# New orders in the hand-over from the output projection to the FFN, and split weights kept for both token halves

## The chip, the cores and the metric

The kernel runs on one core of one Trainium2 chip. The metric is the device time of one execution in microseconds. The core has a matrix engine (PE in the profile, with its weight loads as PEld), a vector engine (DVE), a scalar engine (ACT), a general engine (POOL) and a queue that issues the DMAs (SP). Each runs its own list of instructions in order. They meet only at semaphores, so an instruction that waits holds up all that stands behind it on its engine.

## The reference, cut to what matters

One decoder layer for a prompt of 1024 new tokens (with 16 meta tokens before them) and 8 sample tokens: retention and convolution run in parallel, and one output projection joins them. What follows is where the change lies:

```
mix = concatenate([ret_out, conv_out]) @ w_out          # 1024 x 1024
h   = h + rms_norm(mix, n_mix_post)
xf  = rms_norm(h, n_ffn_pre)
gate, up = split(xf @ w_ffn_in)                         # 1024 x 2*2816
h   = h + rms_norm((silu(gate) * up) @ w_ffn_out, n_ffn_post)
```

Everything is float32.

## The kernel before

**Products.** A float32 product is made of three passes: each operand is split into a rounded part (hi) and a remainder (lo), and hi·hi, hi·lo and lo·hi are added up (`three_pass`, L461 to L463). ACT makes a hi part by a copy, DVE (or POOL) the lo part by a subtraction. The FFN's product of a 2x2 block is made with seven products in place of eight, of sums and differences of blocks. So there are seven weight operands and seven operands of x for each pair of weight blocks. The sums of the weights are made by POOL from the raw weights (`w_sums`).

**Stages.** The FFN runs in 11 groups. Group 0 starts while the output projection still works, and this stage, the hand-over, is what the change touches. The 1032 output tokens are nine tiles: 0 to 7 of 128 tokens, and 8, the samples. Their order is 0, 1, 8, 2, 3, 4, 5, 6, 7, and o is a tile's place in it. The FFN treats the tokens as two halves: ss=0 is made of tiles 0 to 3 and half the samples, ss=1 of tiles 4 to 7 and the rest.

For each tile:

- PE makes the projection, `out_tok(t, 0)` and `out_tok(t, 1)`: 24 matmuls of 512 columns each. (Tiles 0, 1 and 8 come by another way, `mix_back`.)
- ACT squares and sums it (`mix_sum`, L1204). DVE makes mean plus epsilon (`mix_var`, L1703), POOL the power -0.5 (`mix_power`, L688), and DVE scales (`mix_scale`, L1712) into the only buffer `m_sc`.
- POOL adds it to h (`h_add`, L860) in a ring of three buffers, `h_ring`, which SP fills with x ahead and stores to memory afterwards. SP loads the tile at place o+2 only when `h_scale` of place o-1 is done.
- ACT sums the squares of h (`h_sum`, L1204), DVE makes `h_var` (L1719), POOL `h_power` (L688), and DVE `h_scale` (L1727) into the only buffer `h_sc`.
- PE transposes (`h_back`, L2299) into the only PSUM pair for that. It waits until the tile before has been read out of there.
- ACT copies x to `x_a` and splits it (L1234 to L1249), DVE makes the lo parts and two of the sums (`x_own_lo`, L1739 to L1749, and `x_sums_lo`, L1758), and POOL the other two sums (`x_sums_14`, L775 and L776). An even tile is only copied and split. The sums are made when its odd partner is there.

**The order** is written out by hand, one list for each engine. After the last projection PE runs `h_back(6)`, then the seven products of group 0 for ss=0 (k = -7 to -1), `h_back(7)`, and the same seven for ss=1 (k = 0 to 6). Products 7 to 13 (both halves) belong to the second weight block (e=1) and 14 to 20 to the down projection.

**Weights.** The seven split operands of e=0 are made for k = -7 to -1 in a ring of four slots, and then once more for k = 0 to 6 in a ring of seven (`w_op_hi` on ACT, L1265, and `w_op_lo` on DVE, L1763). The raw weights of e=1 of group 0 have buffers of their own, `f_first`, and so have their sums, `t_first`. SP loads them after the last projection (L598).

**Between products** there are partial results: `u2` (L1777) is needed by the product with p=3, and `u3` (L1783), the second gate (L1787), the second up half (L1794) and their product (L1800), the first up half (L1806) and its product (L1815) stand between the weight splits on DVE.

## Time and profile before

| | us |
|---|---|
| median of the runs (three: 1169.47, 1173.04, 1173.50) | 1173.04 |
| the profiled execution, its time | 1173.48 |
| its span | 1171.7 |
| PE busy | 1138.5 |
| DVE busy | 805.4 |
| POOL busy | 610.4 |
| ACT busy | 440.7 |

PE works 97% of the span, so the time can only fall where PE waits or where it runs at the lower of its two clocks. The profile's forty slices show a dip of PE in slices 14 to 17, which is 380 to 500 us. There lies the hand-over. Times of day below are microseconds from the span's start.

### The profile page before, as it was taken

How to read it: one execution, taken by the hardware profiler on the slowest of the kernel's cores; microseconds unless marked ns; L12 is line 12 of the kernel's file. 1: busy time of each engine (PE TensorE's matmuls, PEld its weight loads, DVE VectorE, ACT ScalarE, POOL GpSimd, SP SyncE). 2: the span in 40 equal slices, each digit the busy share in tenths (PEclk: the TensorE clock that was granted, in tenths of full speed). 3: DMA queues.
4: the chain of work that ended last, by engine and by line, in shares of the span. 5: the costliest groups of instructions: out<-in, count | busy, mean ns of one | idle time of the engine just before them, and what ended most of it. 6: DMA issues, size and time to landing. Idle time of an engine off the chain costs nothing.

```text
span 1171.7 us, 22760 instructions
## 1 busy us (share of the span) xinstructions
PE 1138.5 (97%) x8585; PEld 1116.4 (95%) x8585; DVE 805.4 (69%) x1243; ACT 440.7 (38%) x803; POOL 610.4 (52%) x458
## 2 busy tenths in 40 slices
PE   8999999999999988699999999999999999999997
PEld 8999999999999867699999999999999999999997
DVE  6368999954566365768685859594949586867646
ACT  6444444233346434442423333333333333333313
POOL 2066888304123464546565647474747373737416
PEclk9999999999999998899999999999999999999999
DMA  9311111111162431112121111212121212121134
GB/s 316 95 39 53 39 52 55 37 51 53 37 179 64 158 125 54 54 55 73 37 71 37 49 59 37 71 36 72 36 72 36 72 36 72 36 70 37 54 144 165
DMA packets 102360, 84.51 MB, mean 72 GB/s; under 512 B 2723, under 2 KB 89379, under 8 KB 102299
## 3 DMA queue, kind: packets, MB, share of 16 engines
q1 hardware_dynamic: 102258, 83.68, 22.9%
q8 instruction: 36, 0.59, 0.2%
q14 instruction: 18, 0.14, 0.0%
q10 hardware_dynamic: 48, 0.10, 0.0%
HBM read 72.86 MB, written 11.38 MB: 72 GB/s over the span
## 4 chain that ended last, share of the span: by engine, by line
PE 80%; POOL 6%; DVE 6%; issue 4%; DMA 2%; ACT 1%; DVEq 0%; POOLq 0%; SPq 0%; ACTq 0%
PE ps L461 25%; PE ps L463 25%; PE ps L462 24%; DVE w_ring L1763 2%; DMA f_raw<-in_w_ffn_in 2%; POOL st L688 1%; POOL o_last L933 1%; PE ps L2097 1%; DVE ffn_acc L1941 1%; POOL f_sum L804 1%; POOL f_sum L802 1%; POOL h_ring L860 1%; PE ps L2225 1%; POOL f_raw L805 1%; PE ps L2169 1%
## 5 line engine op out<-in xcount | busy, mean ns | idle before, releaser
L1941 DVE TENSOR_TENSOR ffn_acc<-ps,ffn_acc 128x516 f32<-128x516 f32 x264 | 183.7, 696 | 8.7 <-PE ps L463 2.9
L461 PE MATMUL ps<-xn_hi,w_hi 128*128 128x350 f32 (+2 forms) x576 | 187.2, 325 | 0.9 <-DVE xn_lo L1445 0.9
L463 PE MATMUL ps<-xn_lo,w_hi 128*128 128x350 f32 (+2 forms) x576 | 185.2, 322 | 0.0
L462 PE MATMUL ps<-xn_hi,w_lo 128*128 128x350 f32 (+2 forms) x576 | 185.0, 321 | 0.0
L461 PE MATMUL ps<-x_both,w_ring 128*128 128x256 f32 x616 | 173.3, 281 | 6.9 <-DVE e_s L1777 4.2
L461 PE MATMUL ps<-x_hi,w_ring 128*128 128x260 f32 x616 | 175.2, 284 | 4.6 <-DVE e_s L1777 2.5
L463 PE MATMUL ps<-x_lo,w_ring 128*128 128x260 f32 x616 | 174.6, 283 | 0.0
L462 PE MATMUL ps<-x_hi,w_ring 128*128 128x260 f32 x616 | 174.6, 283 | 0.0
L462 PE MATMUL ps<-x_both,w_ring 128*128 128x256 f32 x616 | 174.5, 283 | 0.0
L463 PE MATMUL ps<-x_both,w_ring 128*128 128x256 f32 x616 | 174.3, 283 | 0.0
L461 PE MATMUL ps<-act_hi,w_ring 128*128 128x258 f32 x560 | 158.2, 282 | 0.5 <-DVE e_s L1806 0.4
L462 PE MATMUL ps<-act_hi,w_ring 128*128 128x258 f32 x560 | 158.0, 282 | 0.0
L463 PE MATMUL ps<-act_lo,w_ring 128*128 128x258 f32 x560 | 157.9, 282 | 0.0
L1763 DVE TENSOR_TENSOR w_ring<-f_raw,w_ring 128x512 fp32r<-128x512 f32 x140 | 108.9, 796 | 55.8 <-ACT w_ring L1265 55.1
L1265 ACT CAST w_ring<-f_raw 128x512 fp32r<-128x512 f32 x160 | 96.9, 618 | 123.4 <-POOL f_raw L813 83.2
L688 POOL TENSOR_TENSOR st<-st,nhalf 128x1 f32<-128x1 f32 (+4 forms) x54 | 37.6, 697 | 184.6 <-DVE st L1663 59.9
L461 PEld LDWEIGHTS ps<-x_both,w_ring 128*128 128x128 f32 x616 | 117.6, 191 | 7.4 <-DVE w_ring L1763 4.5
L461 PEld LDWEIGHTS ps<-x_hi,w_ring 128*128 128x128 f32 x616 | 116.9, 190 | 6.5 <-DVE w_ring L1763 5.0
L463 PEld LDWEIGHTS ps<-x_both,w_ring 128*128 128x128 f32 x616 | 117.3, 190 | 0.0
L462 PEld LDWEIGHTS ps<-x_both,w_ring 128*128 128x128 f32 x616 | 116.7, 189 | 0.0
L463 PEld LDWEIGHTS ps<-x_lo,w_ring 128*128 128x128 f32 x616 | 116.6, 189 | 0.0
L462 PEld LDWEIGHTS ps<-x_hi,w_ring 128*128 128x128 f32 x616 | 116.5, 189 | 0.0
(272 smaller groups left out, 2714.1 us busy)
## 6 DMA issues: line engine op xcount, KB each, us to landing
f_raw<-in_w_ffn_in SPq DMA_DIRECT2D x42, 512.0 KB, 3.9
raw<-in_w_in SPq DMA_DIRECT2D x24, 512.0 KB, 3.7
f_raw<-in_w_ffn_out SPq DMA_DIRECT2D x22, 512.0 KB, 3.5
x_st<-in_x_prompt SPq DMA_DIRECT2D x8, 512.0 KB, 7.7
h_ring<-in_x_prompt SPq DMA_DIRECT2D x8, 512.0 KB, 3.8
h_scratch<-h_ring SPq DMA_DIRECT2D x8, 512.0 KB, 3.9
h_fin<-h_scratch SPq DMA_DIRECT2D x8, 512.0 KB
out<-o_last SPq DMA_DIRECT2D x7, 512.0 KB
```

Of the source, the lines that this page charges most:

```text
L461: nc.tensor.matmul(out, hi, mhi, start=first, stop=False, skip_group_check=resumes)
L462: nc.tensor.matmul(out, lo, mhi, start=False, stop=False, skip_group_check=resumes)
L463: return nc.tensor.matmul(out, hi, mlo, start=False, stop=last, skip_group_check=resumes)
L688: g.tensor_tensor(dst, src, nhalf[0:src.shape[0], 0:src.shape[1]], ALU.pow).then_inc(done, 1)
L802: g.tensor_tensor(t3, up[:, half:D], up[:, 0:half], ALU.subtract).then_inc(s_T, 1)
L804: g.tensor_tensor(t2, t3, gate[:, 0:half], ALU.add).then_inc(s_T, 1)
L805: g.tensor_tensor(up[:, 0:half], up[:, 0:half], gate[:, 0:half], ALU.subtract).then_inc(s_T, 1)
L860: g.tensor_tensor(h[o % 3][0:n, :], h[o % 3][0:n, :], m_sc[0:n, :], ALU.add).then_inc(s_h, 1)
L933: g.tensor_tensor(o_last[0:n, t, :], o_last[0:n, t, :], h_fin[t][0:n, :], ALU.add).then_inc(s_y, 1)
L1265: s.copy(w_slot(k, 0), w_op(k, first)).then_inc(s_ohi, 1)
L1763: v.tensor_tensor(w_slot(k, 1), w_op(k, first), w_slot(k, 0).bitcast(F32), ALU.subtract).then_inc(s_olo, 1)
L1941: v.tensor_tensor(a, tile_banks(i), a, ALU.add).then_inc(s_acc, 1)
```

## The change

It leaves all groups from the second on as they are, and changes the hand-over:

- All four lists (PE, DVE, ACT, POOL) are in new orders. The steps on x are cut into smaller ones (`x_first`, `x_even`, `x_odd`; `x_even_lo`, `x_sum_3`, `x_sum_2`, `x_odd_lo`; `x_sum_1`, `x_sum_4`) so that each can have its own place. `MIX_SUMS_BEFORE` and `H_SUMS_BEFORE` hold how many sums come ahead of each.
- PE: the first product stands ahead of `h_back(6)`, and the last two of ss=0 stand behind `h_back(7)`.
- The seven split operands of e=0 are kept for both halves: four in the ring's slots, three in `w_keep`. Products 0 to 6 use them again. Seven copies on ACT and seven subtractions on DVE fall away.
- `f_first` and `t_first` are gone. The raw weights of e=1 come by the ordinary buffers, and their loads wait until the seventh lo part is made.
- The four sums of the first weights (`first_sum`) stand singly between the early additions on POOL.
- The waits on the gains stand one step later. `gate2` and `up2` are steps of their own. The splits for k = 8 to 12 come between the last partial results of e=0.

```diff
-MIX_AHEAD = 3
-CATCH_UP = {7: (10, 11), 8: (12, 13), 9: (14, 15), 10: (16,), 11: (17,), 12: (18,), 13: (19,)}
+KEEP = 7 - MIX_RING
+MIX_SUMS_BEFORE = (3, 3, 4, 5, 5, 6, 7, 8, 9)
+H_SUMS_BEFORE = (0, 0, 0, 2, 3, 5, 6, 7, 8)
...
+        def w_slot(k, part, first=False):
+            if first and k < 7:
+                p = k % 7
+                return (w_ring[p] if p < MIX_RING else w_keep[p - MIX_RING])[:, part, :]
+            return w_ring[k % RING][:, part, :]
...
-                if o == 7:
-                    sp.wait_ge(s_mT, 9)
-                    sp.wait_ge(fraw_in[0], 16)
-                    load_first(0)
-                    load_first(1)
...
                     sp.wait_ge(s_olo, splits(0, 6))
+                    load_gate_up(2, 0, 1, 0)
+                    load_gate_up(0, 0, 1, 1)
                     load_down_half(1, 0, 0)
...
             def p1_copy(g, e, first, k):
                 for ss in subs_of(first, k):
                     act.wait_ge(s_pd, products(g, k, ss, first))
+                    if first and e:
+                        act.wait_ge(s_p2, ss + 1)
...
             out_tok(7, 0)
             out_tok(7, 1)
+            product(0, -7, True)
             h_back(6)
-            for k in range(-7, 0):
-                product(0, k, True)
+            product(0, -6, True)
+            product(0, -5, True)
+            product(0, -4, True)
+            product(0, -3, True)
             h_back(7)
+            product(0, -2, True)
+            product(0, -1, True)
+            product(0, 0, True)
```

The order on DVE before, from the lo part of the fifth weight operand to the last `h_scale` (names: `w_ring` and `w_keep` hold split weights, `e_s` partial results, `x_both` the split x of the second half, `x_f` its sums, `m_sc` the scaled projection, `h_sc` the scaled h):

```order
L1763 TENSOR_TENSOR w_ring_107<-f_raw,w_ring_107 128x512 [waits ffn_w_hi]
L1777 TENSOR_TENSOR e_s_60<-ps,e_s_59 128x260 [waits p1_copied,ffn_products_done]
L1763 TENSOR_TENSOR w_ring_108<-f_raw,w_ring_108 128x512 [waits ffn_w_hi]
L1758 TENSOR_TENSOR x_both_58<-x_f_55,x_both_57 128x1024 [waits x_sums_hi,x_sums_1_4]
L1763 TENSOR_TENSOR w_ring_109<-f_raw,w_ring_109 128x512 [waits ffn_w_hi]
L1783 TENSOR_TENSOR e_s_61<-ps,e_s_59 128x260 [waits ffn_products_done]
L1787 TENSOR_TENSOR e_s_59<-ps,e_s_61 128x260 [waits u3_done]
L1719 TENSOR_SCALAR st<-st 128x1 [waits h_sumsq]
L1763 TENSOR_TENSOR w_ring_106<-f_raw,w_ring_106 128x512 [waits ffn_w_hi]
L1794 TENSOR_TENSOR e_s_61<-ps,e_s_61 128x260 [waits ffn_products_done]
L1800 TENSOR_TENSOR ffn_acc<-e_s_61,e_s_59 128x260 [waits up2_done,gate2_silu]
L1727 SCALAR_TENSOR_TENSOR h_sc<-h_ring_83,st,gain_fp 128x1024 [waits h_transposed,h_rstd]
```

The same place in the change:

```order
L1753 TENSOR_SCALAR st<-st 128x1 [waits mix_sumsq]
L1832 TENSOR_TENSOR w_ring_110<-f_sum,w_ring_110 128x512 [waits ffn_w_hi]
L1832 TENSOR_TENSOR w_keep_78<-f_raw,w_keep_78 128x512 [waits ffn_w_hi]
L1764 SCALAR_TENSOR_TENSOR m_sc<-ps,st,gain_mp 128x1024 [waits h_done,mix_rstd]
L1846 TENSOR_TENSOR e_s_60<-ps,e_s_59 128x260 [waits p1_copied,ffn_products_done]
L1792 TENSOR_TENSOR x_both_58<-ps,x_both_57 128x1024 [waits x_first_half_copied,xf_hi_done]
L1852 TENSOR_TENSOR e_s_61<-ps,e_s_59 128x260 [waits ffn_products_done]
L1827 TENSOR_TENSOR x_both_58<-x_f_55,x_both_57 128x1024 [waits x_sums_hi,x_sums_1_4]
L1771 TENSOR_SCALAR st<-st 128x1 [waits h_sumsq]
L1858 TENSOR_TENSOR e_s_59<-ps,e_s_61 128x260 [waits u3_done]
L1866 TENSOR_TENSOR e_s_61<-ps,e_s_61 128x260 [waits u3_done,ffn_products_done]
L1779 SCALAR_TENSOR_TENSOR h_sc<-h_ring_84,st,gain_fp 128x1024 [waits h_transposed,h_rstd]
```

The wait on the squares of h (`h_sumsq`) had six rows of weight splits, sums and partial results between it and the last x split (`x_both_58<-x_f_55`). Now it stands right behind that split, and two partial results stand between it and the `h_sc` row. The splits of the last two operands (`w_keep_79`, `w_keep_80`) follow after.

DVE before, from the first sums of the last tile on:

```order
L1758 TENSOR_TENSOR x_both_58<-x_f_56,x_both_57 128x1024 [waits x_sums_hi]
L1758 TENSOR_TENSOR x_both_58<-x_f_56,x_both_57 128x1024 [waits x_sums_hi,x_sums_1_4]
L1806 TENSOR_TENSOR e_s_60<-ps,e_s_60 128x260 [waits ffn_products_done]
L1815 TENSOR_TENSOR e_s_60<-e_s_60,ffn_acc 128x260 [waits up1_done,gate1_silu]
L1763 TENSOR_TENSOR w_ring_109<-f_sum,w_ring_109 128x512 [waits ffn_w_hi]
L1763 TENSOR_TENSOR w_ring_110<-f_raw,w_ring_110 128x512 [waits ffn_w_hi]
L1777 TENSOR_TENSOR e_s_60<-ps,e_s_59 128x256 [waits p1_copied,ffn_products_done]
L1763 TENSOR_TENSOR w_ring_111<-f_raw,w_ring_111 128x512 [waits ffn_w_hi]
L1763 TENSOR_TENSOR w_ring_112<-f_raw,w_ring_112 128x512 [waits ffn_w_hi]
L1783 TENSOR_TENSOR e_s_61<-ps,e_s_59 128x256 [waits ffn_products_done]
```

The same place in the change:

```order
L1827 TENSOR_TENSOR x_both_58<-x_f_56,x_both_57 128x1024 [waits x_sums_hi]
L1881 TENSOR_TENSOR e_s_60<-ps,e_s_60 128x260 [waits ffn_products_done]
L1846 TENSOR_TENSOR e_s_60<-ps,e_s_59 128x256 [waits p1_copied,ffn_products_done]
L1827 TENSOR_TENSOR x_both_58<-x_f_56,x_both_57 128x1024 [waits x_sums_hi,x_sums_1_4]
L1832 TENSOR_TENSOR w_ring_107<-f_raw,w_ring_107 128x512 [waits ffn_w_hi]
L1852 TENSOR_TENSOR e_s_61<-ps,e_s_59 128x256 [waits ffn_products_done]
L1858 TENSOR_TENSOR e_s_59<-ps,e_s_61 128x256 [waits u3_done]
L1889 TENSOR_TENSOR e_s_60<-e_s_60,ffn_acc 128x260 [waits up1_done,gate1_silu]
L1866 TENSOR_TENSOR e_s_61<-ps,e_s_61 128x256 [waits u3_done,ffn_products_done]
L1832 TENSOR_TENSOR w_ring_108<-f_sum,w_ring_108 128x512 [waits ffn_w_hi]
L1881 TENSOR_TENSOR e_s_60<-ps,e_s_60 128x256 [waits ffn_products_done]
```

The partial result for the fourth product of the second half (`e_s_60<-ps,e_s_59 128x256`) stood behind two weight splits and the second x split. Now it stands ahead of that x split, and no weight split of e=0 is left.

DVE at the start of the hand-over, before:

```order
L1712 SCALAR_TENSOR_TENSOR m_sc<-ps,st,gain_mp 128x1024 [waits mix_rstd]
L1712 SCALAR_TENSOR_TENSOR m_sc<-ps,st,gain_mp 128x1024 [waits h_done,mix_rstd]
L1719 TENSOR_SCALAR st<-st 128x1 [waits h_sumsq]
L1727 SCALAR_TENSOR_TENSOR h_sc<-h_ring_81,st,gain_fp 128x1024 [waits h_rstd]
L1712 SCALAR_TENSOR_TENSOR m_sc<-ps,st,gain_mp 8x1024 [waits h_done,mix_rstd]
L1719 TENSOR_SCALAR st<-st 128x1 [waits h_sumsq]
L1703 TENSOR_SCALAR st<-st 128x1 [waits mix_sumsq]
L1719 TENSOR_SCALAR st<-st 8x1 [waits h_sumsq]
L1712 SCALAR_TENSOR_TENSOR m_sc<-ps,st,gain_mp 128x1024 [waits h_done,mix_rstd]
```

And in the change:

```order
L1764 SCALAR_TENSOR_TENSOR m_sc<-ps,st,gain_mp 128x1024 [waits gains_in,mix_rstd]
L1753 TENSOR_SCALAR st<-st 128x1 [waits mix_sumsq]
L1753 TENSOR_SCALAR st<-st 8x1 [waits mix_sumsq]
L1764 SCALAR_TENSOR_TENSOR m_sc<-ps,st,gain_mp 128x1024 [waits h_done,mix_rstd]
L1771 TENSOR_SCALAR st<-st 128x1 [waits h_sumsq]
L1764 SCALAR_TENSOR_TENSOR m_sc<-ps,st,gain_mp 8x1024 [waits h_done,mix_rstd]
L1771 TENSOR_SCALAR st<-st 128x1 [waits h_sumsq]
L1753 TENSOR_SCALAR st<-st 128x1 [waits mix_sumsq]
L1764 SCALAR_TENSOR_TENSOR m_sc<-ps,st,gain_mp 128x1024 [waits h_done,mix_rstd]
L1771 TENSOR_SCALAR st<-st 8x1 [waits h_sumsq]
L1779 SCALAR_TENSOR_TENSOR h_sc<-h_ring_82,st,gain_fp 128x1024 [waits h_rstd]
```

The first `h_sc` row stood behind two `m_sc` rows, and now stands behind four.

## Rows read from the trace of the kernel before

**Rows 1.** The page: PE's busy time, and its clock in forty slices (9: full).

```profile
PE 1138.5 (97%) x8585; PEld 1116.4 (95%) x8585; DVE 805.4 (69%) x1243; ACT 440.7 (38%) x803; POOL 610.4 (52%) x458
...
PEclk9999999999999998899999999999999999999999
```

**Rows 2.** Busy time by stretch: us, then PE, PEld, DVE, ACT, POOL; clock; DMA.

```profile
384.40:406.50 22.10, 22.10 (x99) 18.05 (x97) 9.17 (x12) 7.72 (x14) 13.38 (x12) 1.00 0.53 170
406.50:443.30 36.80, 32.37 (x162) 26.11 (x160) 23.61 (x29) 13.63 (x24) 22.72 (x17) 1.00 0.31 100
443.30:468.40 25.10, 21.22 (x89) 17.25 (x89) 13.13 (x16) 11.20 (x17) 10.45 (x9) 0.86 0.17 63
468.40:504.40 36.00, 26.58 (x185) 25.95 (x184) 26.88 (x37) 16.35 (x29) 14.74 (x9) 0.86 0.18 59
504.40:545.00 40.60, 39.66 (x331) 39.31 (x330) 32.58 (x51) 13.08 (x27) 29.84 (x23) 1.00 0.18 52
545.00:1140.00 595.00, 593.26 (x4940) 591.56 (x4940) 415.05 (x702) 195.27 (x390) 336.75 (x253) 1.00 0.18 56
```

**Rows 3.** What PE waited for, 380 to 545 us: total, times, longest.

```profile
PE ps L461 <- DVE e_s L1777: 6.7, 2, 4.2
PE ps L2299 <- DVE h_sc L1727: 3.9, 1, 3.9
PE ps L461 <- DVE x_both L1758: 2.7, 1, 2.7
PE ps L2299 <- issue: 2.5, 1, 2.5
PE ps L2299 <- DVE x_lo L1749: 1.9, 2, 1.4
```

**Rows 4.** PE's timeline: first matmul of out_tok(4, 0), h_back(1), out_tok(4, 1).

```profile
407.37 0.48 PE L461 MATMUL ps<-w_hi,mix 128*128 128x512 f32 x1
...
412.94 1.03 PE L2299 MATMUL ps<-t_sm,h_sc 128*128 128x128 f32 x8
413.73 0.48 PE L461 MATMUL ps<-w_hi,mix 128*128 128x512 f32 x1
```

**Rows 5.** DVE's timeline, and POOL's: start, length, line, operation.

```profile
392.81 3.42 DVE L1727 SCALAR_TENSOR_TENSOR h_sc<-h_ring,st,gain_fp 128x1024 f32<-128x1024 f32 x1 [0.67 <-POOL st L688]
...
392.73 2.41 POOL L860 TENSOR_TENSOR h_ring<-h_ring,m_sc 128x1024 f32<-128x1024 f32 x1
```

**Rows 6.** Lengths of single steps: h_add, x_sum, power (POOL); x_lo (DVE).

```profile
413.14 2.38 POOL L860 TENSOR_TENSOR h_ring<-h_ring,m_sc 128x1024 f32<-128x1024 f32 x1 [3.43 <-DMA h_ring<-in_x_prompt]
...
419.49 1.27 POOL L775 TENSOR_TENSOR x_sum<-x_sum,x_a 128x512 f32<-128x512 f32 x1 [0.99 <-DVE x_sum L1748]
...
453.93 0.55 POOL L688 TENSOR_TENSOR st<-st,nhalf 128x1 f32<-128x1 f32 x1 [1.46 <-DVE st L1703]
...
435.64 1.21 DVE L1739 TENSOR_TENSOR x_lo<-ps,x_hi 128x1024 fp32r<-128x1024 f32 x1
```

**Rows 7.** Timelines of the last tile: ACT's sum, POOL's power, four of DVE.

```profile
468.61 1.02 ACT L1204 ACTIVATE junk_c<-ps 128x1024 f32<-128x1024 f32 x1 [2.39 <-PE ps L463]
...
469.99 1.48 POOL L688 TENSOR_TENSOR st<-st,nhalf 128x1 f32<-128x1 f32 x1 [6.21 <-DVE st L1703]
...
479.94 0.14 DVE L1719 TENSOR_SCALAR st<-st 128x1 f32<-128x1 f32 x1
...
481.83 1.28 DVE L1727 SCALAR_TENSOR_TENSOR h_sc<-h_ring,st,gain_fp 128x1024 f32<-128x1024 f32 x1
...
487.29 1.32 DVE L1758 TENSOR_TENSOR x_both<-x_f,x_both 128x1024 fp32r<-128x1024 f32 x1 [0.51 <-ACT x_both L1243]
...
496.85 0.41 DVE L1777 TENSOR_TENSOR e_s<-ps,e_s 128x256 f32<-128x256 f32 x1
```

**Rows 8.** SP's timeline: the fourth load of x, the loads of f_first.

```profile
396.25 0.33 SPq L582 DMA_DIRECT2D h_ring<-in_x_prompt  x1
...
468.60 1.01 SPq L598 DMA_DIRECT2D f_first<-in_w_ffn_in  x2
```

More of the change, by code:

```diff
@@ L806, in w_sums @@
                 pool.wait_ge(s_T, 4 * i + 3)
-                if e and not first:
+                if e:
                     pool.wait_ge(s_olo, splits(gg, 7 * e))
-                elif not first:
+                else:
                     act_lo_of(gg - 1, 7, 1, e_s2[:, :])
@@ L813, in w_sums @@
                 g.tensor_tensor(t4, gate[:, half:D], t2, ALU.subtract).then_inc(s_T, 1)
-                if e == 0 and not first:
+                if e == 0:
                     w_op_lo(gg, 1)
@@ L1345, in _ @@
             act.wait_ge(s_wlo, SLOTS + N_IN + N_OUT)
-            for o in range(3):
-                mix_sum(o)
+            mix_sum(0)
+            mix_sum(1)
+            mix_sum(2)
             h_sum(0)
@@ L1787, in u3, with up2 @@
                     v.tensor_tensor(e_s1[:, c], ps[:, 5 + 2 * ss, 0:SUBW[ss]], e_s3[:, c], ALU.add).then_inc(s_c21, 1)
-            def act2(g, e, first, k, last):
-                dst = e_s3 if e or last else side(first)
+            def up2(g, e, first, k):
                 for ss in subs_of(first, k):
@@ L1793, in act2 @@
                     dve.wait_ge(s_pd, products(g, k, ss, first))
+                    if first and e == 0:
+                        dve.wait_ge(s_s3, ss + 1)
                     v.tensor_tensor(e_s3[:, c], ps[:, 1 + 2 * ss, 0:SUBW[ss]], e_s3[:, c], ALU.add).then_inc(s_c22, 1)
+            def act2(g, e, first, k, last):
+                dst = e_s3 if e or last else side(first)
                 for ss in subs_of(first, k):
@@ L1808, in act1 @@
             def act1(g, e, first, k):
-                up1(g, e, first, k)
                 for ss in subs_of(first, k):
@@ L1823, in product_step @@
                 e, p = part_of(k)
-                if k == 7 or k == 0 and first:
+                if k == 7 and not first:
+                    up1(g, 0, first, k - 1)
                     act1(g, 0, first, k - 1)
@@ L1846, in _ @@
             mix_var(3)
+            mix_scale(3)
             h_var(2)
-            mix_scale(3)
-            h_var(3)
+            h_scale(0)
             h_scale(1)
             mix_var(4)
+            x_even_lo(0)
+            h_var(3)
             mix_scale(4)
-            x_own_lo(0)
+            x_sum_3(1)
+            x_sum_2(1)
+            h_scale(2)
+            x_odd_lo(1)
             h_var(4)
-            h_scale(2)
-            x_own_lo(1)
+            x_sums_lo(1, 0)
+            h_scale(3)
@@ L1857, in _ @@
+            x_even_lo(8)
             mix_var(5)
-            h_scale(3)
+            x_sum_3(8)
+            x_sum_2(8)
+            x_odd_lo(8)
             mix_scale(5)
-            x_own_lo(8)
-            x_sums_lo(1, 0)
             x_sums_lo(1, 1)
+            h_scale(4)
+            x_even_lo(2)
+            h_var(5)
             x_sums_lo(8, 0)
             x_sums_lo(8, 1)
-            h_scale(4)
-            x_own_lo(2)
-            h_var(5)
+            h_scale(5)
             mix_var(6)
-            h_scale(5)
+            x_sum_3(3)
@@ L1870, in _ @@
             mix_scale(6)
-            x_own_lo(3)
-            x_own_lo(4)
+            x_sum_2(3)
+            x_odd_lo(3)
+            h_var(6)
+            h_scale(6)
+            x_even_lo(4)
             x_sums_lo(3, 0)
             x_sums_lo(3, 1)
-            h_var(6)
-            h_scale(6)
+            x_sum_3(5)
             mix_var(7)
+            x_sum_2(5)
             mix_scale(7)
-            x_own_lo(5)
+            x_odd_lo(5)
+            w_op_lo(0, -7, True)
+            w_op_lo(0, -6, True)
@@ L1899, in _ @@
             x_sums_lo(7, 0)
+            up1(0, 0, True, -1)
+            u2(0, 0, True, 1, False)
             x_sums_lo(7, 1)
+            w_op_lo(0, 7, True)
+            u3(0, 0, True, 3)
+            gate2(0, 0, True, 3)
+            act1(0, 0, True, -1)
+            up2(0, 0, True, 4)
+            w_op_lo(0, 8, True)
+            up1(0, 0, True, 6)
+            act1(0, 0, True, 6)
+            act2(0, 0, True, -3, False)
+            w_op_lo(0, 9, True)
+            w_op_lo(0, 10, True)
+            w_op_lo(0, 11, True)
@@ L1902, in out_var @@
+            w_op_lo(0, 12, True)
+            act2(0, 0, True, 4, False)
             def out_var(o):
@@ L1927, in ffn_group @@
             def ffn_group(g, first=False):
-                for k in range(14):
+                for k in range(7 if first else 0, 14):
                     product_step(g, k, first)
@@ L2413, in ffn_group @@
             def ffn_group(g, first=False):
-                for k in range(14):
+                for k in range(7 if first else 0, 14):
                     product(g, k, first)
```

287 lines of the change are left out of this document (173 added, 114 removed).

## The prediction

> **What bounds the kernel now.** I read the page first. PE is busy 97% of the span and its clock is full but for five slices [rows 1]. So the time falls only where PE waits or runs slowly. The busy times by stretch say where that is. From 545 to 1140 us PE is idle for 1.7 us in all, and from 504.4 to 545 for 0.9. In the hand-over, from the first projection of tile 2 (384.4) to the first product of the second weight block (504.4), it is busy 102.3 of 120.0 us, with the clock at 0.86 of full from 443.3 on [rows 2]. The list of waits fills the idle 17.7 us: 11.0 before transposes and products that lack h or x, and 6.7 before products that wait for a partial result, u2, or for what lies around it on DVE [rows 3].
>
> What must PE do there? A projection half takes 5.57 us, and the transposes of a tile 0.79 [rows 4]. A product of twelve matmuls takes 1.44, since the later groups run 4940 matmuls in 593.3 us [rows 2]. Twelve halves are 66.8, nine transposes about 7.0, fourteen products 20.2: **94.0 us**. So the hand-over could end at 384.4 + 94.0 = 478.4. It ends at 504.4. Of the 26.0 us between, 17.7 are idle and 8.3 (102.3 - 94.0) are work at the lower clock, 1.2 GHz in place of 2.4. That is the most that new orders can bring.
>
> **The early part of the change.** I went through the new lists by hand, each step at the later of its engine being free and its sources being ready, with the durations of rows 4 to 7. The first additions wait for x, as before. `h_scale` of the first tile now stands behind four `m_sc` rows and ends at about 402.4, not 396.2, so SP's load of the fourth tile is issued there and not at 396.25 [rows 8]. Some 4 us of transfer make `h_add(3)` start at 406.5. Nobody is late by it: PE transposes that tile only from 425.5 on, and needs the first at 406.6.
>
> From there on the question at each transpose is whether the scaled h is there and the tile before has been read out. In the new lists the lo parts and sums of tile 1 no longer wait for the squares of tile 3, and the weights' first sums (four on POOL) are done before 405, where POOL was free, and no longer stand in the middle of the stage before a power (one sum has the length of an x sum, 1.27 [rows 6]). My times by which everything is ready, against the time at which PE gets there, are: sample tile 417.4 against 419.4, tile 2 422.4 against 425.6, tile 3 431.1 against 431.8, tile 4 437.5 against 438.0, tile 5 444.2 against 444.4. An example, tile 5: `h_add(6)` ends at 438.6, two x sums on POOL of 1.27 each end at 441.1, the power at 441.7, `h_scale` (1.28) at 443.0, `x_even_lo(4)` (1.21) at 444.2 [rows 6, 7]. So the idle of 1.9, 2.5 and 3.9 us [rows 3] goes, and so does the stretch at the lower clock that followed [rows 2]. The last three margins are under 1 us, though.
>
> **The last tile of h.** PE ends the projection at 456.3 in this count. The chain from there to the last `h_scale` holds ACT's two sums (1.25 with the read-out of the sum, each), two means (0.14), two powers (0.55), two scalings (1.28) and `h_add` (2.4): 8.8 us [rows 6, 7]. Before, it took 14.5 (468.6 to 483.1), since the power took 1.48 and the second mean ran only at 479.94, behind weight splits and partial results [rows 7]. In the new order it stands behind one x split. I add 0.9 for nine hand-overs by semaphore of 0.1, 0.6 for a power that meets a weight split, and 0.9 for two partial results ahead of `h_scale`: 11.2. PE covers of it one product, one transpose and four products, 1.44 + 0.79 + 5.76 = 8.0, and 0.5 of a wait for u2 among them. **A gap of 2.7 us is left** ahead of the last transpose, and 0.5 for u2. For both I keep 1 to 6.
>
> **The last tile of x.** Before, PE had one product to do while the sums of tile 7 went through DVE, ACT and DVE, and waited 2.7; then the u2 of the second half stood behind splits and PE waited 4.2 [rows 3, 7]. Now three products (4.3 us) cover the first, which takes some 4.0: the scaled h was there at 483.1, a product's rest and the transposes took until about 484.6, and the x split that PE waits for ended at 488.6 [rows 7], and the u2 stands ahead of the last x split. The wait of 2.5 in the first half was for a split of a reused slot with a scaling in front; those splits now come ahead. All 9.4 go.
>
> **Weights kept.** Seven copies of 0.52 on ACT and seven subtractions of 0.7 on DVE fall away, 4.9 us of DVE. None is added to the sum: they lay in the stretch whose waits are already counted. They are the reason why those waits can go.
>
> **The second block's weights** come later. Their loads left at 468.6, early enough to be no part of any wait [rows 8]. Now they leave after the seventh lo part, at about 469 in my count, when the rest of the kernel is 23 us earlier. Landing (4.6), two sums (2.6), a copy and a split (1.3) end by 479.7 with the queues between them; the product that needs them starts at 484. That is a margin of 4 us. The next partial result, u2 of the second block, needs products, `act2` behind four weight splits and two POOL steps: about 488 to 489.5 against 489.9. So I charge nothing, and up to 2 in the range.
>
> **The shared path of DVE and POOL.** A row shows what can spoil the margins. An `h_scale` started 0.1 us after an `h_add` on POOL and took 3.42 us in place of 1.28: it ended 1.1 after the addition did [rows 5]. The two ran one after the other. The Trainium skill (SBUF — State Buffer, "Who interferes with whom") says the same: a DVE instruction with two SBUF inputs and a GpSimd instruction that reads SBUF exclude each other for their whole length. The row agrees. Between 406.5 and 468.4 POOL was busy 33.2 us of 61.9 [rows 2]. In the new orders this part has 50 us. It holds on POOL five additions (12.0), eight x sums (10.2) and ten powers (5.5), and on DVE seven scalings (9.0), four x splits of 1.2 and two weight splits (6.3) that read SBUF twice: 43 us for the path. At 0.87 load a step will often meet another. I let them meet where my count showed it, and put **2.5 us** for the rest into the sum (0 to 6).
>
> **The clock.** The stretches with gaps of 2.5 to 4.2 us ran at 0.86 of the clock, while the one before, with gaps of 0.5 to 2.5, ran at full clock [rows 2, 3]. For a remaining gap near 3 us I take **1.3**, with 0 to 3.
>
> **The sum.** 26.0 available, less 3.2, 2.5 and 1.3: 19.0 us. 1173.48 - 19.0 = 1154.5 for an execution like the profiled one. The median lies 0.4 below it, so I take **1154.0**. This likeliest case reaches from 1150 to 1158.
>
> **Rivals.**
>
> 1. *The shared path sets the pace.* The five transposes of tiles 3 to 7 each come late by one blocked step (1.2 us), and the gap before the last grows by 2: 8.0 us of waiting in place of 2.5, and the lower clock costs 4.3 in place of 1.3. The gain is 26.0 - 3.2 - 8.0 - 4.3 = 10.5: 1162.5. For it: three margins under 1 us, and the load of 0.87. Against it: in the trace most DVE steps that read PSUM ran beside POOL unharmed, and the waits before were due to order. By the rule of the SBUF page alone this would be the outcome. Chance 0.25.
> 2. *Everything fits.* The gap at the last transpose shrinks to 1 and the clock stays full: 1148.5. Chance 0.15.
> 3. *The ring of h becomes the pacemaker, and the kernel slower.* The new order delays `h_scale(0)` by 6.2 us and with it a load. If each of the six later tiles waited as long as the fourth's addition (4.0 us), 24 us would be lost against 19.0 gained: 1178. It decides from 3.2 us for each tile on. Against it: the next loads leave at 409, 416.7 and 421.7 in my count, and the additions that need them start at 413, 425 and 436, each after at least the 4 us that a load takes. Chance 0.03.
> 4. *The second block's weights come late.* Landing and sums behind the x sums on POOL take 10 us longer than I count, PE waits 6 before the block's second product and falls to the lower clock for 2 to 3: about 1162.5. Chance 0.07.
> 5. *The orders do little:* PE waits elsewhere for the same 17.7 us, since some step in order holds a list up that I took for ready. 1168 to 1174. Chance 0.05.
>
> The forecast has the remaining 0.45. A measurement here can tell about 0.5% (5.9 us) from no change. Faster by more than that (under 1167.2) are the forecast, rivals 1, 2 and 4 and a part of 5: 0.92. Within it 0.05, slower 0.03. The range that leaves out 2 in 10 is 1148 to 1163: rivals 1, 2 and 4 end just within it.
>
> **What the new profile would show.** PE's idle before transposes and products should fall from 17.7 to 3 to 6 us between the first projection of tile 2 and the second block, and the first product of the second block should start near 485 (504.4 before). The longest wait should be that for `h_sc` before the last transpose, 2 to 4 us. No wait for u2 over 1 us should be left. The clock should be full until about 465. The stretches after it should be as long as before. I am wrong if waits at the transposes of tiles 3 to 5 remain (rival 1), if PE waits before the first down product or the second block's products (rival 4), or if later groups take longer.

## The result, and the profile after

The changed kernel takes **1151.67 us** (median of 4 runs, 1151.47 to 1151.94), against 1173.27 us for the kernel before, measured beside it (median of 4; one of the four took 2865.26, and the median of the other three is 1173.04). The ratio is 0.9827 with a 95% interval of 0.9804 to 0.985: faster by 21.6 us. The forecast was 1154.0, with a range of 1148 to 1163. The profiled execution took 1151.94 us with a span of 1150.1. A later set on one chip gave 1151.69 us (5 runs, label `after_again`), and its hand-over takes 99.2 us in both traces. So differences of about 1 us between kernels can be read below, where their runs don't overlap.

The page of the kernel after, with PE's busy time and its clock in forty slices (9 is full), answers to [rows 1]:

```profile
PE 1132.0 (98%) x8585; PEld 1111.5 (97%) x8585; DVE 797.8 (69%) x1236; ACT 436.5 (38%) x796; POOL 605.3 (53%) x458
...
PEclk9999999999999999999999999999999999999999
```

The busy times by stretch answer to [rows 2]. The columns are the stretch, its length, then PE, PEld, DVE, ACT and POOL, the clock, and DMA's share and rate. The stretch that ends at 483 holds about the work of the one that ended at 504.4 before:

```profile
384.40:406.50 22.10, 22.10 (x103) 18.04 (x101) 10.33 (x12) 7.26 (x14) 15.78 (x14) 1.00 0.46 146
406.50:443.30 36.80, 36.80 (x187) 30.42 (x186) 21.72 (x32) 18.05 (x30) 20.86 (x17) 1.00 0.41 138
443.30:468.40 25.10, 22.86 (x138) 20.02 (x137) 20.53 (x28) 14.42 (x24) 10.85 (x8) 1.00 0.13 52
468.40:483.00 14.60, 13.93 (x105) 13.75 (x104) 10.97 (x15) 5.37 (x10) 9.64 (x6) 0.88 0.37 109
483.00:545.00 62.00, 60.94 (x507) 60.41 (x508) 46.60 (x77) 21.47 (x44) 36.14 (x27) 1.00 0.17 52
```

What PE waited for from 380 to 545 us, in total, how often and the longest, answers to [rows 3]:

```profile
PE ps L2407 <- DVE h_sc L1779: 2.2, 1, 2.2
PE ps L462 <- DVE e_s L1866: 1.2, 2, 0.7
PE ps L462 <- DVE e_s L1881: 0.4, 1, 0.4
```

Between 406.5 and 443.3 PE is now never idle; there it lost 4.4 us before. The list of waits holds 3.8 us up to 545. In the kernel before it holds 18.6: the 17.7 of [rows 3], all ahead of 504.4, and two of 0.5 and 0.4 behind it. The largest is the one before the last transpose, and the clock is below full only after it. PE's timeline shows the start of the stage, that transpose, the matmuls behind it (0.42 us each in place of 0.28, at the lower of the two clock levels), and the first product of the second weight block:

```profile
385.16 0.47 PE L462 MATMUL ps<-w_hi,mix 128*128 128x512 f32 x1
...
468.16 1.42 PE L2407 MATMUL ps<-t_sm,h_sc 128*128 128x128 f32 x8 [2.25 <-DVE h_sc L1779]
469.58 0.42 PE L463 MATMUL ps<-x_hi,w_keep 128*128 128x260 f32 x1
...
484.36 0.28 PE L462 MATMUL ps<-x_hi,w_ring 128*128 128x260 f32 x1
```

**Where the 21.6 us came from.** The hand-over, from the first projection of tile 2 to the first product of the second weight block, takes 99.2 us (385.16 to 484.36), and took 120.0: 20.8 less. PE is idle in it for 2.9 (2.25 and 0.67) in place of 17.7, which gives 14.8. It is busy for 96.3 in place of 102.3, which gives 6.0: the lower clock cost 8.3, and now costs about 14.6 x 0.12 = 1.8. The hand-over begins 0.8 later than before, at 385.16; in the other traces of the changed kernel and its variants it begins between 384.5 and 385.9, so this is about the scatter between executions. All that follows the hand-over takes 665.7 in place of 667.3, 1.6 less, of which 1.1 is idle time of PE (2.7 against 1.6, without the last 32 us). 20.8 - 0.8 + 1.6 is the 21.6 between the two spans.

### The profile page after: what moved, and what is told of

Read it like the earlier page. It is cut to its first block, busy times and chain, and to the rows that moved or that the text cites. A ratio compares the mean times of both kernels' runs of the same rounds, so it can differ in the third digit from the quotient of the medians.

```text
span 1150.1 us, 22756 instructions
## 1 busy us (share of the span) xinstructions
PE 1132.0 (98%) x8585; PEld 1111.5 (97%) x8585; DVE 797.8 (69%) x1236; ACT 436.5 (38%) x796; POOL 605.3 (53%) x458
## 4 chain that ended last, share of the span: by engine, by line
PE 87%; DVE 5%; POOL 3%; DMA 2%; issue 2%; ACT 1%; DVEq 0%; SPq 0%; POOLq 0%; ACTq 0%
PE ps L462 27%; PE ps L464 27%; PE ps L463 27%; DVE w_ring L1832 2%; DMA f_raw<-in_w_ffn_in 1%; POOL o_last L955 1%; PE ps L2204 1%; PE ps L2407 1%; PE ps L2332 1%; PE ps L2276 1%; PE ps L2333 1%; POOL st L682 1%; DMA x_st<-in_x_prompt 1%; PE ps L2223 1%; DVE ffn_acc L2047 0%
## 5 line engine op out<-in xcount | busy, mean ns | idle before, releaser
L462 PE MATMUL ps<-x_hi,w_ring 128*128 128x260 f32 x604 | 170.9, 283 | 1.1 <-DVE e_s L1866 0.7
L464 PE MATMUL ps<-x_lo,w_ring 128*128 128x260 f32 x604 | 170.5, 282 | 0.0
L463 PE MATMUL ps<-x_hi,w_ring 128*128 128x260 f32 x604 | 170.4, 282 | 0.0
L463 PE MATMUL ps<-x_both,w_ring 128*128 128x256 f32 x604 | 170.0, 281 | 0.0
L464 PE MATMUL ps<-x_both,w_ring 128*128 128x256 f32 x604 | 169.7, 281 | 0.0
L462 PE MATMUL ps<-x_both,w_ring 128*128 128x256 f32 x604 | 168.4, 279 | 0.0
L1832 DVE TENSOR_TENSOR w_ring<-f_raw,w_ring 128x512 fp32r<-128x512 f32 x137 | 106.5, 795 | 57.4 <-ACT w_ring L1297 56.6
L462 PEld LDWEIGHTS ps<-x_hi,w_ring 128*128 128x128 f32 x604 | 113.9, 189 | 2.9 <-issue 1.7
L462 PEld LDWEIGHTS ps<-x_both,w_ring 128*128 128x128 f32 x604 | 114.1, 189 | 0.0
L464 PEld LDWEIGHTS ps<-x_both,w_ring 128*128 128x128 f32 x604 | 113.8, 188 | 0.0
L464 PEld LDWEIGHTS ps<-x_lo,w_ring 128*128 128x128 f32 x604 | 113.6, 188 | 0.0
L463 PEld LDWEIGHTS ps<-x_hi,w_ring 128*128 128x128 f32 x604 | 113.5, 188 | 0.0
L1832 DVE TENSOR_TENSOR w_ring<-f_sum,w_ring 128x512 fp32r<-128x512 f32 x54 | 55.5, 1041 | 83.5 <-ACT w_ring L1297 83.5
```

Of the source, the lines that this page charges most:

```text
L462: nc.tensor.matmul(out, hi, mhi, start=first, stop=False, skip_group_check=resumes)
L463: nc.tensor.matmul(out, lo, mhi, start=False, stop=False, skip_group_check=resumes)
L464: return nc.tensor.matmul(out, hi, mlo, start=False, stop=last, skip_group_check=resumes)
L1832: v.tensor_tensor(w_slot(k, 1, first), w_op(k, first), w_slot(k, 0, first).bitcast(F32), ALU.subtract).then_inc(s_olo, 1)
```

## The experiments

Every time is a median of several runs, measured in rounds with the kernel before on the same chip. "+5.0" is against the changed kernel's 1151.7. Where the length of the hand-over is given, it is that of the profiled execution, from the first projection of tile 2 to the first product of the second block.

**1. One part alone, on the kernel before: the partial result u2 ahead of the last x split** (`a1_u2_alone`). It takes up the largest wait of [rows 3].

```
-                if p == 1:
+                if p == 1 and not (first and k == 1):
...
             x_sums_lo(7, 0)
+            u2(0, 0, True, 1, False)
             x_sums_lo(7, 1)
```

> The kernel before, with one part of the change alone: on DVE the partial result u2 of the second half (ss=1) stands ahead of the last x split of tile 7 instead of behind two weight splits. Theory A (orders and kept weights belong together): ACT's copy that u2 reads still stands behind a weight copy, and the fourth weight operand is split right behind u2, so PE's wait of 4.2 us shrinks by 1 to 2.5 us only, and the time falls to 1170.5 to 1172.5. Theory B (the place of u2 alone makes the wait): the 4.2 us go, and with them the slow stretch after, 1166 to 1169.

Measured: 1172.43 us, ratio 0.9996 (0.9986 to 1.0005). No change: Theory B is out, and of theory A the shorter wait isn't there either. The head of its list of waits:

```profile
PE ps L461 <- DVE w_ring L1763: 4.8, 1, 4.8
PE ps L461 <- DVE x_both L1758: 2.7, 1, 2.7
PE ps L461 <- DVE e_s L1777: 2.5, 1, 2.5
```

The wait of 4.2 for u2 is gone, and one of 4.8 for a weight split stands in its place. DVE's timeline in that kernel shows the split for which PE waits, 1.75 us long, behind the partial results:

```profile
490.11 0.42 DVE L1777 TENSOR_TENSOR e_s<-ps,e_s 128x256 f32<-128x256 f32 x1 [3.13 <-ACT e_s L1270]
...
493.16 1.75 DVE L1763 TENSOR_TENSOR w_ring<-f_sum,w_ring 128x512 fp32r<-128x512 f32 x1
```

So on the old orders this step shortened nothing: the weights are split again there, behind it. u2 itself also waited 3.1 us for ACT's copy.

**2. The same step, taken out of the changed kernel** (`t1_u2_behind_splits`).

```
-            u2(0, 0, True, 1, False)
             x_sums_lo(7, 1)
             w_op_lo(0, 7, True)
+            u2(0, 0, True, 1, False)
```

> The changed kernel, but the u2 of the second half of the products stands behind the last x split and the split of weight 7, instead of ahead of both. In the trace of the changed kernel these two ran from 477.07 to 480.66 us (1.90 and 1.77), and PE begins the product that needs u2 at about 477.9. Theory A (that place in the order is needed, although the same move in the kernel before brought nothing): PE waits 3.2 us there, of which the two waits of 0.7 and 0.5 behind it may take up a part; 2.5 to 3.5 us slower than the changed kernel, 1154.2 to 1155.2. Theory B (the place doesn't matter in the new order either): within 0.5 us of it.

Measured: 1154.9 us (1154.46 to 1155.86), +3.2. Theory A holds: PE waits 3.4 for u2 (forecast 3.2), and one of the two waits of the changed kernel behind it, that of 0.7, is gone. PE's timeline and DVE's:

```profile
481.18 0.36 PE L462 MATMUL ps<-x_both,w_ring 128*128 128x256 f32 x1 [3.39 <-DVE e_s L1846]
...
476.95 2.08 DVE L1827 TENSOR_TENSOR x_both<-x_f,x_both 128x1024 fp32r<-128x1024 f32 x1 [2.94 <-ACT x_both L1279]
478.96 1.75 DVE L1832 TENSOR_TENSOR w_ring<-f_raw,w_ring 128x512 fp32r<-128x512 f32 x1
480.62 0.41 DVE L1846 TENSOR_TENSOR e_s<-ps,e_s 128x256 f32<-128x256 f32 x1
```

A step that is worth nothing on the kernel before is worth 3.2 us in the new one. Together with experiment 1 this says that its place pays only where what comes behind it is ready too.

**3. The old orders up to tile 5, the new ones from there on** (`h1_old_head`). The lists of DVE, ACT and POOL up to the splits of tile 5 are those of the kernel before; the rest, the kept weights and PE's list are the new ones. The head of POOL's list shows the kind of edit:

```
             h_add(0)
-            h_add(1)
             h_power(0)
-            first_sum(0)
+            h_add(1)
             h_add(2)
-            mix_power(3)
             h_power(1)
-            first_sum(1)
+            mix_power(3)
...
```

> The changed kernel, with the lists of DVE, ACT and POOL in the order of before up to tile 5 (including the first weights' sums after the fifth addition), and the new lists from the weight splits on. PE's list as changed. Theory A (the order of the early part brings its own share): the waits at the transposes of tiles 2, 3 and 5 return with 7 to 8 us and a slow stretch of 2 to 3 behind them, 1160.5 to 1163.5. Theory B (what the early part loses is given back, since PE's last products would only wait less later): the last transpose's wait of 2.2 goes and the rest is 4 to 6, 1155 to 1158.

Measured: 1163.9 us (1161.76 to 1164.63), +12.2, just above the range of theory A; theory B is out. So the new orders of the early part bring more than half of the gain, 12.2 of 21.6 us on top of the rest. (What the single steps cost when taken out, here and below, overlaps and can't be added up.) The waits are those of [rows 3] again, at the transposes:

```profile
PE ps L2407 <- DVE h_sc L1779: 6.1, 2, 3.9
PE ps L2407 <- DVE x_lo L1817: 2.9, 3, 1.4
PE ps L2407 <- issue: 1.4, 1, 1.4
...
443.30:468.40 25.10, 20.33 (x86) 16.30 (x85) 12.22 (x17) 11.58 (x17) 11.90 (x9) 0.86 0.17 63
```

The list of waits sums to 12.0 us against 3.8, and the clock is 0.86 from 443.3 to 468.4, as it was before. The hand-over takes 110.6 us.

**4. Is it the first sums of the weights?** The prediction laid the wait of 2.5 us at a transpose to four additions on POOL. Here the changed kernel has them back at their old place (`a3_first_sums_late`).

```
             h_power(0)
-            first_sum(0)
             h_add(2)
...
             h_add(5)
+            first_sum(0)
+            first_sum(1)
+            first_sum(2)
+            first_sum(3)
             h_power(5)
```

> The changed kernel, with the four sums of the first weights on POOL together behind the fifth h_add again, ahead of the power for tile 4, as before. Theory A (as the prediction had it: these sums made the power, and with it a transpose, late): the transpose of tile 4 comes 1 to 3 us late, with a wait for h_sc in PE's list, 1153 to 1155.5. Theory B (the power has room, since its h_scale waits for PE's transpose before it anyway): 0 to 1 us, 1151.5 to 1152.7.

Measured: 1152.53 us (1151.33 to 1153.35). Its waits are 2.2, 1.2 and 0.4 us, the same as in the changed kernel, and none is at a transpose of tiles 3 to 5. The hand-over takes 99.3 us against 99.2. Theory B holds: in the new orders the place of the first sums brings nothing that can be measured. What the wait of 2.5 us was is read from the trace of the kernel before, in the section on why the prediction was right.

**5. Is anybody late by the first scaled h?** It goes back to its old place in the list, ahead of `mix_scale(2)` (`a4_first_h_early`).

```
             h_var(0)
+            h_scale(0)
             mix_scale(2)
...
-            h_scale(0)
             h_scale(1)
```

> The changed kernel, with h_scale of the first tile put back right behind its mean, so that SP's fourth load of x leaves about 8 us earlier. Theory A (nothing hangs on that load): no wait of PE changes, within 0.6 us of 1151.7. Theory B (a late load is passed on through the ring of h to the last tile): the wait before the last transpose shrinks, 1 to 2 us faster. The h_scale took 4.6 us in the changed kernel where three operations of POOL followed each other; alone with one addition it should take 1.3 to 3.5.

Measured: 1152.02 us (1151.41 to 1153.07), no change, with the same waits and a hand-over of 99.2 us, although SP's load of the fourth tile left at 398.25 instead of 405.88. The delay is harmless, as forecast.

**6. Two products ahead of the last transpose instead of behind it** (`a2_last_transpose_late`).

```
-            h_back(7)
             product(0, -2, True)
             product(0, -1, True)
+            h_back(7)
```

> The changed kernel, with PE's products k = -2 and -1 put back ahead of the last transpose, as before the change; all other lists as changed. Theory A (what follows the last transpose is a fixed chain of about 4 us, and these two products are its cover): PE waits for the weight splits behind the last h_scale, and then again 2 to 3 us for the x sums of tile 7: 2 to 4 us slower than the change, 1153.7 to 1155.7. Theory B (the place does not matter, since PE waits the same time at another point): within 1 us of 1151.7.

Measured: 1156.63 us (1155.86 to 1156.96), +5.0, more than I expected. PE's timeline has a gap ahead of the product in front of the transpose, and one behind the transpose:

```profile
468.54 0.58 PE L462 MATMUL ps<-x_hi,w_keep 128*128 128x260 f32 x1 [2.85 <-DVE w_keep L1832]
...
477.95 0.36 PE L462 MATMUL ps<-x_both,w_ring 128*128 128x256 f32 x1 [2.69 <-DVE x_both L1827]
```

The products cannot fill the gap, since the kept weights they need are split behind the last `h_scale` on DVE, and then only one product is left to cover the sums of tile 7. The idle time grows by 2.6 (6.4 against 3.8). The clock falls to 0.78 from 468.4 to 483, which costs 1.5 us more than 0.88 does. That accounts for some 4 of the 5.0.

**7. What the kept weights save DVE** (`b1_seven_more_splits`). Seven subtractions of the length of a weight split are added on DVE, on a spare buffer, around the places where the second pass of weights 0 to 6 used to be split.

```
             up2(0, 0, True, -3)
+            again(1)
             h_scale(8)
             w_op_lo(0, -2, True)
+            again(1)
             w_op_lo(0, -1, True)
+            again(1)
...
             up1(0, 0, True, -1)
+            again(2)
             u2(0, 0, True, 1, False)
             x_sums_lo(7, 1)
+            again(1)
             w_op_lo(0, 7, True)
+            again(1)
```

> The changed kernel, with seven subtractions of 512 columns more on DVE (into a spare buffer, of the size of the weight splits that the change saves), spread from ahead of the last h_scale to behind the last x split; they wait only for one another. Theory A (the kept weights bring their time only where their splits stood in a chain: one ahead of h_scale, two ahead of the sums of tile 7, the others in gaps): 1.5 to 3 us slower, 1153.2 to 1154.7. Theory B (DVE has room, kept weights bring nothing): under 0.7 us. Theory C (DVE is the bound there): all of 7 x 0.69 = 4.8 us and more.

Measured: 1153.84 us (1152.83 to 1154.89), +2.2. One subtraction stands ahead of the last `h_scale`, and the wait for it is 2.8 in place of 2.2; the other waits together are 3.0 in place of 1.6:

```profile
PE ps L2422 <- DVE h_sc L1781: 2.8, 1, 2.8
PE ps L464 <- DVE e_s L1868: 2.1, 2, 1.6
```

Alone, seven such steps take 4.8 us; here they took 7.7, as three of them ran beside POOL. They cost 2.2 us, as theory A has it. That is the price of DVE's time at these places. ACT's seven copies and the order of slots that they would need were not put back.

**8. The second block's weights 7 us later** (`b2_second_block_late`). SP's loads wait for one more product.

```
                     sp.wait_ge(s_olo, splits(0, 6))
+                    sp.wait_ge(s_pd, products(0, 1, 1, True))
                     load_gate_up(2, 0, 1, 0)
```

> The changed kernel, with the loads of the second block's raw weights held back until PE's second product of the second half is done, 7 us later (469.3 to 476.5). Theory A (the second block has a margin of about 4 us at its second product, and only 1 us at its u2, which hangs on act2 behind four weight splits): PE waits 2.5 to 4.5 us more, mainly for u2 before the fourth product of the block, 1154.2 to 1157. Theory B (7 us are covered): within 1 us of 1151.7.

Measured: 1156.62 us (1156.14 to 1157.46), +5.0. The loads leave at 476.08 instead of 469.33, 6.75 later. Rows of SP, ACT, DVE and PE, in this order, show what happens:

```profile
476.08 1.01 SPq L586 DMA_DIRECT2D f_raw<-in_w_ffn_in  x2
...
479.99 0.62 ACT L1298 CAST w_ring<-f_raw 128x512 fp32r<-128x512 f32 x1 [4.99 <-DMA f_raw<-in_w_ffn_in]
480.51 1.04 ACT L1280 CAST x_both<-x_f 128x1024 fp32r<-128x1024 f32 x1
...
481.65 1.22 DVE L1828 TENSOR_TENSOR x_both<-x_f,x_both 128x1024 fp32r<-128x1024 f32 x1 [5.19 <-ACT x_both L1280]
...
483.02 0.55 PE L462 MATMUL ps<-x_both,w_keep 128*128 128x256 f32 x1 [4.20 <-DVE x_both L1828]
```

The time is in the range of theory A, but its reason is wrong: PE did not wait for a product of the second block. ACT's copy of the first late weight stands in ACT's list ahead of the copy of the last x sum, which the first block needs. ACT waits there for the transfer, and the x sum waits behind it. PE's waits sum to 7.3 us against 3.8, and the clock, full in the changed kernel from 483 to 504.4, is 0.86 there.

In this run, where ACT waits for the transfer, the copy starts 3.9 us after the loads were issued (476.08 to 479.99). In the changed kernel it starts at 475.40, 6.07 us after them. So the slack on ACT is about 2.2 us there, not the 4 that the prediction counted at PE.

**9. Filling the remaining gap** (`i1_product_in_gap`). One product moves ahead of the last transpose, and on DVE the weight splits that it needs move ahead of an x split. PE's part:

```
+            product(0, -2, True)
             h_back(7)
-            product(0, -2, True)
```

> A version meant to be faster than the change: the product k = -2 stands ahead of the last transpose; on DVE mix_scale(8) comes ahead of the fifth weight split, the sixth is made ahead of the last h_var, and the x split of tile 5 that stood ahead of that mean comes behind h_scale(8). Theory A (the wait of 2.2 us before the transpose is the chain's, shorter by 0.6 with the new order, and the product fills the rest; the wait moves to the product that needs the sums of tile 7, but is shorter, and the slow stretch of 1.3 us goes): PE waits 1 to 2 us in all, 1149.5 to 1151.0. Theory B (the chain's end is fixed and the slow stretch comes with any gap): within 0.6 us of 1151.7.

Measured: 1151.04 us (1150.58 to 1152.14), within the spread of the changed kernel, so the time decides between neither theory. The gap of 2.25 at the transpose became 0.28, and PE waited 1.12 and 0.65 for kept weights and 0.8 for an x split instead. Its waits sum to 4.2 us, more than the 3.8 of the changed kernel and than the 1 to 2 of theory A. What did change is the clock: it was at 1.00 throughout. The hand-over takes 98.9 us against 99.2.

**10. The same, with three steps of DVE sooner** (`i2_sooner_splits`).

```
             x_even_lo(6)
+            w_op_lo(0, -3, True)
+            w_op_lo(0, -2, True)
             u3(0, 0, True, -4)
...
             h_scale(8)
-            w_op_lo(0, -2, True)
             w_op_lo(0, -1, True)
+            x_sums_lo(5, 1)
...
+            up2(0, 0, True, 4)
             act1(0, 0, True, -1)
-            up2(0, 0, True, 4)
```

> The kernel with one product moved ahead of the last transpose, with three steps of DVE moved as well: two kept weights are split before u3 instead of behind it, the last kept one before the x split of tile 4, and the up half is added before the last multiplication of the sample rows. In the trace of the version before it PE waited 1.12 and 0.65 us for kept weights and 0.5 and 0.9 us for these additions. Theory A (each of these waits was due to the order on DVE alone): about 1.5 us go, 1149.5 us. Theory B (the engines behind them are the limit, a wait reappears one step later at x_both or h_sc): no change, 1150.7 to 1151.5 us.

Measured: **1150.1 us** (1150.01 to 1150.73, ratio 0.9814), against 1151.69 (1151.05 to 1152.75) for the changed kernel beside it. The runs of the two don't overlap: 1.6 us faster, and the fastest version of this study. That lies between the two theories (1149.5, and 1150.7 to 1151.5). PE's list of waits and the stretch behind the transpose:

```profile
PE ps L462 <- DVE x_both L1827: 1.6, 1, 1.6
PE ps L462 <- DVE e_s L1866: 0.5, 1, 0.5
PE ps L462 <- DVE e_s L1881: 0.4, 1, 0.4
PE ps L2407 <- DVE h_sc L1779: 0.3, 1, 0.3
...
468.40:483.00 14.60, 12.96 (x110) 12.79 (x109) 11.73 (x16) 6.84 (x13) 10.19 (x6) 1.00 0.36 109
```

PE is idle for 2.8 us in place of 3.8, no stretch is below full clock, and the hand-over takes 97.0 us in place of 99.2. What is left is the chain of tile 7's sums, with two products to cover it.

**11. The changed kernel again** (`after_again`), for the comparison in 2 and 10.

> The changed kernel itself, run beside the next two on the same chip so that differences under 0.2% can be read. Expected: 1151.7 us, as before (1151.47 to 1151.94).

Measured: 1151.69 us, as before.

## Why the prediction was right

**The bound held.** PE works without a gap where x and h allow it, and the second block's first product starts at 484.36 (forecast 485) though the stage began 0.76 later than the prediction assumed. From 385.16 that is 99.2 us: the 94.0 of work, 2.9 of idle (2.25 and 0.67), 1.8 of lower clock, and 0.5 that the count of work lacked.

**Early part, transposes of tiles 3 to 5: right in sum, wrong in one reason.** PE reaches them at 432.89, 439.26 and 445.73, 1.1 to 1.3 us after my times for it, and waits at none. For tile 5, DVE's timeline shows how near it was:

```profile
442.85 1.28 DVE L1779 SCALAR_TENSOR_TENSOR h_sc<-h_ring,st,gain_fp 128x1024 f32<-128x1024 f32 x1 [1.67 <-POOL st L682]
444.05 1.22 DVE L1792 TENSOR_TENSOR x_both<-ps,x_both 128x1024 fp32r<-128x1024 f32 x1
```

The lo part ends at 445.27 and PE comes at 445.73, a margin of 0.46 (forecast 0.2). Experiment 3 shows that the early orders carry the effect. The first `h_scale` was forecast to end at 402.4 and ended at 405.85; no wait came of it, and experiment 5 shows that none hangs on it.

The reason given for the wait of 2.5 us, the first sums in the middle of the stage ahead of a power, was wrong. The wait is that of the transpose at 436.95 in the kernel before. Two rows of DVE and one of POOL show what stood ahead of it:

```profile
427.61 5.80 DVE L1758 TENSOR_TENSOR x_lo<-x_sum,x_hi 128x1024 fp32r<-128x1024 f32 x4
433.34 2.38 DVE L1727 SCALAR_TENSOR_TENSOR h_sc<-h_ring,st,gain_fp 128x1024 f32<-128x1024 f32 x1
...
433.34 1.29 POOL L804 TENSOR_TENSOR f_sum<-f_sum,f_raw 128x512 f32<-128x512 f32 x1
```

Four splits of x sums stood on DVE ahead of `h_scale`, 5.80 us in all, though the two long ones take 1.2 each when alone. This then took 2.38 in place of 1.28, beside one of the first sums, and the split that reads the tile before out of PSUM ended at 436.85. In experiment 3 the same four splits take 5.79, `h_scale` takes 1.27 and the wait is 1.4. So the first sums had a part of 1.1 us in it, through the path that DVE and POOL share and not through a power, and the rest was the order on DVE and what the four splits lost beside POOL: the new list has the two sample splits behind `h_scale`. That single move was not tried alone.

**Last tile of h: the chain was 1 us shorter.** The rows of ACT, POOL and DVE that carry it:

```profile
457.89 1.03 ACT L1226 ACTIVATE junk_c<-ps 128x1024 f32<-128x1024 f32 x1 [1.36 <-PE ps L464]
...
459.27 0.93 POOL L682 TENSOR_TENSOR st<-st,nhalf 128x1 f32<-128x1 f32 x1 [2.63 <-DVE st L1753]
...
462.23 2.41 POOL L873 TENSOR_TENSOR h_ring<-h_ring,m_sc 128x1024 f32<-128x1024 f32 x1 [2.03 <-DVE m_sc L1764]
...
466.00 0.15 DVE L1771 TENSOR_SCALAR st<-st 128x1 f32<-128x1 f32 x1
...
466.81 1.28 DVE L1779 SCALAR_TENSOR_TENSOR h_sc<-h_ring,st,gain_fp 128x1024 f32<-128x1024 f32 x1
```

From 457.89 to 468.09 it takes 10.2 us (14.5 in [rows 7], 11.2 forecast). The power meets a weight split and takes 0.93 instead of 0.55; 0.6 was allowed for that. Less the 8.0 that PE covers, the chain leaves 2.2, and the gap was 2.25 (forecast 2.7, and 0.5 for u2, which did not occur). In the list before, three rows stood between the last x split and the mean of h, and three more up to `h_scale`; the six named ahead of the prediction are both together. The 0.67 before the last product was not forecast: the up half's sum stands there behind a multiplication, `act1`. Experiment 10 moved it ahead, and that wait was gone.

**Last tile of x: right, and it depends on the whole.** All 9.4 us went. The wait of 2.5 among them was for the u2 of the first half [rows 3], which stood behind a weight split of 1.94 us (473.83 to 475.77). Experiments 1 and 2 show that the place of u2 is needed (3.2 us) and was not enough.

**Kept weights: right as "no term of their own".** DVE's time for seven splits costs 2.2 us in the new order (experiment 7), and its saving is part of why the waits at the end could go. That is a part of the 9.4 already counted and not added to it.

**Second block's weights: right in the sum, wrong in the place.** There was no wait in the changed kernel. The margin was about 2.2 us at ACT, and what it guards is the first block's x sum (experiment 8).

**Shared path: the term of 2.5 us was mis-sized.** Single steps did meet: the first `h_scale` took 4.60 us and that of the samples 2.01 (both in the last section), and the last x split and the weight split behind it took 1.90 and 1.77. But no transpose came late by one in the early part, so the term measured nothing there. This is the largest single miss. The slips fell where the list had slack. Rival 1 would have shown waits at the transposes of tiles 3 to 7, and there is one only, at the last, where the chain's own length accounts for it.

**The clock: 1.8 us against 1.3.** Its place was as forecast, behind the gap at the last transpose.

Set against the sum: 26.0 less 2.9 of idle, 1.8 of clock and 0.5 of uncounted work leaves 20.8 in the hand-over, where the forecast was 19.0. Too much were the 2.5 for the shared path and 0.3 of idle, too little 0.5 of clock and the 0.5 of work. The 1.6 behind the hand-over and the 0.8 of its later start were in no term, and together they add 0.8 to the 20.8: that part of the 21.6 was not foreseen.

## What to carry to other kernels

Where PE waits in a stage and each wait has another cause, first work out how long PE's own work is from the row of one step: that floor, with the length of the last dependent chain, gave the time here within 0.3%, with the misses of the last paragraph in it. Test a reordering as a whole. A single move that names the largest wait may bring nothing, because the next step in the same list is late by as much, and the same move taken out of the finished order costs 3 us (experiments 1 and 2). When a load or a copy is moved in a list, count the slack at the engine that waits for it first, not at the one that uses the result: what stands behind it in that list is what becomes late.

## What the runs showed of the hardware

**A step of DVE can be passed over several times.** In the changed kernel `h_scale(0)`, which reads two inputs from SBUF, took 4.60 us. DVE's row, and then POOL's rows beside it:

```profile
401.25 4.60 DVE L1779 SCALAR_TENSOR_TENSOR h_sc<-h_ring,st,gain_fp 128x1024 f32<-128x1024 f32 x1
...
400.46 1.29 POOL L796 TENSOR_TENSOR f_sum<-f_sum,f_raw 128x512 f32<-128x512 f32 x1
401.71 0.54 POOL L682 TENSOR_TENSOR st<-st,nhalf 8x1 f32<-8x1 f32 x1
402.23 1.28 POOL L798 TENSOR_TENSOR f_raw<-f_raw 128x512 f32<-128x512 f32 x1
403.48 1.28 POOL L801 TENSOR_TENSOR f_raw<-f_raw,f_sum 128x512 f32<-128x512 f32 x1
```

It ended 1.09 us after the last of four POOL instructions that followed one another without a gap. The prediction had taken one blocked step as one POOL instruction long. With the first sums elsewhere (experiment 4) the same step took 1.26 us:

```profile
400.25 1.26 DVE L1779 SCALAR_TENSOR_TENSOR h_sc<-h_ring,st,gain_fp 128x1024 f32<-128x1024 f32 x1
```

It is not so each time that POOL's instructions follow one another. In the changed kernel the `h_scale` of the samples, with the same two inputs from SBUF, waits for one instruction of POOL only and runs ahead of the next, though that one starts without a gap too. DVE, then POOL:

```profile
416.18 2.01 DVE L1779 SCALAR_TENSOR_TENSOR h_sc<-h_ring,st,gain_fp 8x1024 f32<-8x1024 f32 x1
...
414.71 2.40 POOL L873 TENSOR_TENSOR h_ring<-h_ring,m_sc 128x1024 f32<-128x1024 f32 x1 [0.66 <-DVE m_sc L1764]
417.07 2.28 POOL L768 TENSOR_TENSOR x_sum<-x_sum,x_a 128x512 f32<-128x512 f32 x1
```

The addition ends at 417.11 and DVE's step 1.08 us later, at 418.19. POOL's next instruction, of 1.29 when alone, is the one that is lengthened. What decides between the two outcomes no run here shows. The Trainium skill (SBUF — State Buffer, "Who interferes with whom") calls the shared pair of ports an exclusive lock and has the order of issue decide who blocks. The rows of the samples agree. In those of `h_scale(0)` a step that started at 401.25 ran behind three instructions of POOL that started after it, from 401.71 on, so there the order of issue did not decide.

**The clock and gaps.** The granted clock fell after a gap of 2.25 us in the changed kernel: it is 0.88 over the stretch of 14.6 us, and 0.50, the lower level of 1.2 GHz, from 469 to 472. With the idle time spread over gaps of 1.12 us and less (experiment 9) or of 1.64 and less (experiment 10) it stayed at 1.00. The kernel before has two gaps of 2.5: behind that at 436.95 the clock stays at 1.00 up to the next gap, at 449.9, and behind that at 476.26 it is 0.54 up to 480. So the length of one gap doesn't decide it alone; what does was not tried.
